# Two-layer hybrid decoder trunk with a mixture of experts: router matmuls turned around, top two by pairwise comparison, expert order and slots of the first expert moved ahead

## The reference

```python
def moe_ffn(x, w_router, wg, wu, wd):
    xt = x.reshape(B * S, D)
    logits = (xt @ w_router).astype(jnp.float32)
    top_v, top_i = lax.top_k(logits, TOP_K)
    w = jax.nn.softmax(top_v, axis=-1)
    gates = jnp.sum(jax.nn.one_hot(top_i, N_EXPERTS, dtype=jnp.float32) * w[..., None], axis=1)
    for e in range(N_EXPERTS):
        y = y + gates[:, e:e + 1].astype(xt.dtype) * swiglu(xt, wg[e], wu[e], wd[e])
```

## Time and profile before

| | |
|---|---|
| median of 3 runs | 1472.94 us (1471.33 to 1474.48) |
| the profiled execution's own time | 1472.44 us |
| its span | 1470.7 us |
| PE busy | 1396.2 us, 95% |
| DVE busy | 819.5 us, 56% |
| ACT busy | 705.5 us, 48% |
| DMA | 444.37 MB, mean 302 GB/s |
| chain that ended last | PE 86%, DVE 5%, ACT 4%, DMA 2% |

### The profile page before, as it was taken

How to read it: one execution, slowest core, us unless ns; L and a number is a source line. 1 busy time by engine, 2 the same in 40 slices (tenths; PEclk the granted TensorE clock), 3 DMA queues, 4 the chain that set the end, 5 groups by cost and what they waited for, 6 DMA issues and landing times.

```text
span 1470.7 us, 16634 instructions
## 1 busy us (share of the span) xinstructions
PE 1396.2 (95%) x6613; PEld 1012.9 (69%) x6613; DVE 819.5 (56%) x794; ACT 705.5 (48%) x773; POOL 35.9 (2%) x92
## 2 busy tenths in 40 slices
PE   8989999999899897999999999999999999999995
PEld 6865688888777746675756785757667757666574
DVE  4624454544354246655647675756656846547476
ACT  5454443444253523445635564545446645436363
POOL 2000000000000000000000000000000000000011
PEclk9989999999999897999999999999999999999998
DMA  9630755555343224999999999999999999999993
GB/s 342 224 115 1 258 199 180 192 174 176 137 148 126 104 86 158 410 409 409 402 409 410 403 393 394 409 411 409 409 396 410 410 409 403 409 410 409 402 403 128
DMA packets 148478, 444.37 MB, mean 302 GB/s; under 512 B 9454, under 2 KB 21612, under 8 KB 148396
## 3 DMA queue, kind: packets, MB, share of 16 engines
q1 hardware_dynamic: 146836, 438.24, 77.8%
q0 software_dynamic: 1440, 4.98, 0.8%
q10 hardware_dynamic: 120, 0.04, 0.0%
HBM read 439.30 MB, written 3.93 MB: 301 GB/s over the span
## 4 chain that ended last, share of the span: by engine, by line
PE 86%; DVE 5%; ACT 4%; DMA 2%; issue 1%; POOL 0%; DVEq 0%; POOLq 0%; SPq 0%; ACTq 0%
PE bank L821 83%; PE bank L824 3%; DVE ring_l L1772 1%; ACT part_h L1394 1%; DMA most<-in_moe_w_down_dram 1%; DMA ring<-in_moe_w_down_dram 1%; DVE most_l L1772 1%; DVE part_l L1772 0%; DVE more_l L1772 0%; ACT junk L1403 0%; ACT xh L1394 0%; ACT prob L1595 0%; DVE y L1772 0%; ACT probT L1394 0%; DVE gm L1777 0%
## 5 line engine op out<-in xcount | busy, mean ns | idle before, releaser
L1394 ACT ACTIVATE part_h<-ring 128x2048 fp32r<-128x2048 f32 x144 | 274.1, 1918 | 136.9 <-PE bank L821 132.4
L821 PE MATMUL bank<-part_h,xh 128*128 128x512 f32 x784 | 312.1, 398 | 6.1 <-DVE xl L2180 2.5
L821 PE MATMUL bank<-part_h,xl 128*128 128x512 f32 x784 | 306.2, 391 | 0.0
L1772 DVE TENSOR_TENSOR ring_l<-ring,part_h 128x2048 fp32r<-128x2048 f32 x102 | 231.6, 2289 | 49.5 <-ACT part_h L1394 48.7
L821 PEld LDWEIGHTS bank<-part_h,xh 128*128 128x128 f32 x784 | 147.6, 188 | 46.9 <-issue 8.2
L821 PE MATMUL bank<-part_h,hTh 128*128 128x512 f32 x392 | 156.2, 398 | 17.0 <-DVE ring_l L1772 10.2
L821 PEld LDWEIGHTS bank<-part_h,xl 128*128 128x128 f32 x784 | 147.5, 188 | 31.7
L821 PE MATMUL bank<-part_h,hTl 128*128 128x512 f32 x392 | 153.9, 393 | 0.0
L1772 DVE TENSOR_TENSOR part_l<-ring,part_h 128x2048 fp32r<-128x2048 f32 x42 | 96.1, 2292 | 83.8 <-ACT part_h L1394 83.8
L1772 DVE TENSOR_TENSOR part_l<-part_in,part_h 128x2048 fp32r<-128x2048 f32 x54 | 123.0, 2289 | 32.6 <-ACT part_h L1394 32.1
L821 PE MATMUL bank<-part_l,xh 128*128 128x512 f32 x360 | 140.2, 389 | 0.0
(11 more groups left out here) (320 smaller groups left out, 1837.9 us busy)
## 6 DMA issues: line engine op xcount, KB each, us to landing
ring<-in_moe_w_down_dram SPq DMA_DIRECT2D x60, 1024.0 KB, 13.9
ring<-in_moe_w_up_dram SPq DMA_DIRECT2D x58, 1024.0 KB, 14.7
ring<-in_moe_w_gate_dram SPq DMA_DIRECT2D x50, 1024.0 KB, 12.6
part_in<-in_moe_w_down_dram SPq DMA_DIRECT2D x36, 1024.0 KB, 14.0
most<-in_moe_w_gate_dram SPq DMA_DIRECT2D x27, 1024.0 KB, 14.8
part_in<-in_moe_w_up_dram SPq DMA_DIRECT2D x27, 1024.0 KB, 13.4
part_in<-in_moe_w_gate_dram SPq DMA_DIRECT2D x21, 1024.0 KB, 15.2
most<-in_moe_w_up_dram SPq DMA_DIRECT2D x17, 1024.0 KB, 13.2
```

Of the source, the lines that this page charges most:

```text
L821: return nc.tensor.matmul(o, lhsT, rhs, start=start, stop=stop)
L1394: return nc.scalar.activation(dst, src, ACT.Copy, scale=scale)
L1772: return nc.vector.tensor_tensor(o, a, b, op)
```

## The change

The router's weights, four times side by side and with the norm's gains multiplied in, become the stationary operand `w_r4` (32 columns, made once in the first layer by four VectorE operations); `xT` moves, 256 columns, and the eight products go to four column groups of the array, two into each. Evictions to `xT` are plain copies of 512 columns, two on each engine. The four partial sums are copied to SBUF (`lgT`) and two products with `fold` add them and turn them back. Six products whose result nobody reads stand between (`warm`). The best two of eight are found by comparing every pair of logits (`margin`, `beats`, `above`), without `rs`, which only the gap for the gates gets. Ranks and totals go to banks of their own, with two signals. `first_slots` builds expert 0's `gm` straight from ranks and selection; `gg` is built only for the last expert. The order of experts moves ahead of the first rows, `gates` and the third piece's split behind them, and `gates_shared` behind that. The first piece waits for half of the rows only (`m_xl`). The scaling of `xs` and one of the two squares change place or engine: ScalarE does the scaling, and squares block 0 before it evicts. The exponential moves behind ScalarE's first rows.

TensorE:

```diff
-                if l:
-                    pe.wait_ge(s_xTa, 4 * (3 * l + 2) + 4)
-                    pe.wait_ge(s_xTv, 4 * (3 * l + 2) + 4)
...
+            def warm(count):
+                for _ in range(count):
+                    mm(bank[7][:, :], part_h[:, 0, 0:P], part_h[:, 0, 0:W], True, True)
+            pe.wait_ge(s_wr, 1)
+            pe.wait_ge(s_hi, PIECES + 1)
+            t = 4 * (3 * (L - 1) + 2)
+            for i in range(KT // 2):
+                pe.wait_ge(s_xTv if i % 2 else s_xTa, t + 2 * (i // 2 + 1))
+                for k in (2 * i, 2 * i + 1):
+                    c = 32 * (k % 4)
+                    last = mm(bank[0][c:c + 32, 0:SEQ], w_r4[:, k, :], xT[:, k, :],
+                              k < 4, k >= 4)
+            last.then_inc(s_lp, 1)
+            warm(2)
+            pe.wait_ge(s_lt, 1)
             for b in range(NB):
-                for k in range(KT):
-                    i = mm(bank[0][:, b * E:(b + 1) * E], xT[:, k, b * P:(b + 1) * P], w_r[:, k, :],
-                           k == 0, k == KT - 1)
-            i.then_inc(s_lp, 1)
+                last = mm(bank[1][:, b * E:(b + 1) * E], lgT[:, b * P:(b + 1) * P], fold[:, 0:E], True, True)
+            last.then_inc(s_lp, 1)
+            warm(4)
...
+                    if (part, m) == (0, 0) and i * ks % (KT // 2) == 0:
+                        pe.wait_ge(m_xl, i * ks // (KT // 2) + 1)
```

VectorE (the first lines are in the first layer's mixer):

```diff
+                            for r in range(32 // E):
+                                i = tt(w_r4[:, :, r * E:(r + 1) * E], w_r[:, :, :],
+                                       cols[:, c_:c_ + KT, None].to_broadcast([P, KT, E]), ALU.mult)
+                            i.then_inc(s_wr, 1)
...
+            nc.vector.tensor_copy(lgT, bank[0][:, 0:SEQ]).then_inc(s_lt, 1)
...
+            dve.wait_ge(s_lp, 2)
+            link(nc.vector.tensor_copy(lg[:, :, :].rearrange("p b e -> p (b e)"), bank[1][:, 0:NB * E]))
+            for b in range(NB):
+                i = tt(margin[:, b], lg[:, b, None, :].to_broadcast([P, E, E]),
+                       lg[:, b, :, None].to_broadcast([P, E, E]), ALU.subtract)
+            link(i)
+            for b in range(NB):
+                i = tt(beats[:, b], margin[:, b], rank_hot[:, :, :], ALU.is_ge)
+            link(i)
+            link(nc.vector.tensor_reduce(above[:, :, :], beats, AX_X, ALU.add))
+            ts(rsg[:, 1], above[:, :, :], 2.0, None, ALU.is_lt).then_inc(s_sel, 1)
...
+            def first_slots():
+                dve.wait_ge(s_rk, 1)
+                link(nc.vector.tensor_copy(rsg[:, 0].rearrange("p b e -> p (b e)"), bank[2][:, 0:NB * E]))
+                for b in range(NB):
+                    ts(gm[:, b, :], iota_s[:, :], rsg[:, 0, b, 0:1], rsg[:, 1, b, 0:1],
+                       ALU.is_equal, ALU.mult).then_inc(m_first, 1)
...
+                    if shares:
+                        i = ts(gg[:, b, :], iota_s[:, :], col[:, b:b + 1], col[:, 2 * NB + b:2 * NB + b + 1],
+                               ALU.is_equal, ALU.mult)
...
-            slots(0, experts, m_gm)
+            first_slots()
+            expert_order()
+            moe_rows_low(0, 0)
+            moe_rows_low(0, 1)
+            gates()
             for j in AHEAD[1]:
                 split_moe(j)
-            moe_rows_low(0, 0)
-            moe_rows_low(0, 1)
+            gates_shared()
```

ScalarE:

```diff
                 if l:
-                    turned(3 * l + 2, "ffn", KT * l)
-                    block_squares()
+                    block_squares(0)
+                    turned(3 * l + 2)
+                    block_squares(1)
+                    act.wait_ge(s_xp, XB * (3 * l + 2))
+                    for b in range(NB):
+                        act.wait_ge(s_hrs, NB * l + b + 1)
+                        i = copy(xs[:, b, :], h[:, b, :], rs[:, b:b + 1])
+                    i.then_inc(s_xs, 1)
```

More of the change, by code:

```diff
@@ L15 @@
 NEG = -1e30
-HUGE = 3.0e38
+TINY = 1.2e-38
 NOPE, ROPE, HEADS = 64, 32, 4
@@ L1234, in gather_expert @@
             def gather_expert(e, r):
-                if e == 0 and r == 0:
-                    pe.wait_ge(s_xs, 1)
+                if e == 0:
+                    if r == 0:
+                        pe.wait_ge(s_xs, 1)
+                    for k in range(KT // 2):
+                        for b in range(NB):
+                            if r == 0 and k == 0:
+                                pe.wait_ge(m_first, b + 1)
+                            kk_ = KT // 2 * r + k
+                            last = mm(gather_bank(e, r)[:, k * P:(k + 1) * P], xs[:, b, kk_ * P:(kk_ + 1) * P],
+                                      gm[:, b, :], b == 0, b == NB - 1)
+                    last.then_inc(m_xep, 1)
+                    return
                 if r == 0:
-                    pe.wait_ge(m_gm, e + 1)
+                    pe.wait_ge(m_gm, e)
                 if e == 1:
@@ L1414, in mean_squares, with turned @@
                 squares_done(s_ms)
-            def turned(t, name, first):
-                for k in (0, 1, 4, 5):
+            def turned(t):
+                for k in (0, 4):
                     act.wait_ge(s_xp, XB * t + k // 2 + 1)
-                    copy(xT[:, k, :], bank[FFN_BANK[k // 2]][:, (k % 2) * SEQ:(k % 2 + 1) * SEQ],
-                         columns(name, first + k)).then_inc(s_xTa, 1)
+                    copy(xT[:, k:k + 2, :].rearrange("p k t -> p (k t)"),
+                         bank[FFN_BANK[k // 2]][:, :]).then_inc(s_xTa, 2)
             def split(f, j):
@@ L1832, in group_out, with turned @@
                        ALU.mult).then_inc(s_xTv, 1)
-            def turned(t, name, first):
-                for k in (2, 3, 6, 7):
+            def turned(t):
+                for k in (2, 6):
                     dve.wait_ge(s_xp, XB * t + k // 2 + 1)
-                    ts(xT[:, k, :], bank[FFN_BANK[k // 2]][:, (k % 2) * SEQ:(k % 2 + 1) * SEQ], columns(name, first + k), None,
-                       ALU.mult).then_inc(s_xTv, 1)
+                    nc.vector.tensor_copy(xT[:, k:k + 2, :].rearrange("p k t -> p (k t)"),
+                                          bank[FFN_BANK[k // 2]][:, :]).then_inc(s_xTv, 2)
             for l in range(L):
@@ L2058, in _ @@
                 if l:
-                    turned(3 * l + 2, "ffn", KT * l)
-                    scale_rows(l)
+                    turned(3 * l + 2)
                 else:
@@ new lines, in _ @@
+            link(ts(rank_hot[:, :, :], rank_hot[:, :, :], TINY, None, ALU.mult))
+            dve.wait_ge(s_lp, 2)
[4 more added lines that the diff above has]
+            link(i)
+            for b in range(NB):
+                i = tt(beats[:, b], margin[:, b], rank_hot[:, :, :], ALU.is_ge)
@@ new lines, in _, with gates @@
+            link(i)
+            link(nc.vector.tensor_reduce(above[:, :, :], beats, AX_X, ALU.add))
+            ts(rsg[:, 1], above[:, :, :], 2.0, None, ALU.is_lt).then_inc(s_sel, 1)
+            def gates():
+                for k in range(2):
+                    i = ts(oh[:, k], above[:, :, :], float(k), None, ALU.is_equal)
+                link(i)
+                for k in range(2):
+                    link(tt(rt_a[:, :, :], oh[:, k], lg[:, :, :], ALU.mult))
+                    link(nc.vector.tensor_reduce(top[:, k, :], rt_a[:, :, :], AX_X, ALU.add))
+                link(tt(gd[:, 0, :], top[:, 1, :], top[:, 0, :], ALU.subtract))
+                dve.wait_ge(s_hrs, NB * L)
+                tt(gd[:, 0, :], gd[:, 0, :], rs[:, 0:NB], ALU.mult).then_inc(s_lm, 1)
@@ L2136, in slots @@
+            def slots(n, key, done, shares):
+                n = n - 1
                 ts(eqm[:, :], key, cnt[:, 0:1], None, ALU.is_equal).then_inc(s_col, 1)
@@ L2287, in _ @@
                     dve.wait_ge(m_xep, rounds_before(e))
-                    slots(e, place[:, :], m_gm)
+                    slots(e, place[:, :], m_gm, e == E - 1)
                 if j in WIDE_N and EARLY <= j:
```

128 lines of the change are left out of this document (57 added, 71 removed).

## The result

| | before | changed |
|---|---|---|
| median | 1473.64 us (1471.33 to 1474.48, 4 runs) | 1462.51 us (1461.53 to 1465.13, 4 runs) |
| the profiled execution: own time, span | 1472.44, 1470.7 | 1461.96, 1460.1 |
| ratio, 95% interval | | 0.993 [0.9916, 0.9943] |

The changed kernel is faster by 0.7%. Between the profiled executions it is 10.5 us, where 14.6 were forecast.

A forecast was written before the change was run, and what follows sets the result against it. Near the end DMA decides, just before and after TensorE; the end moves by the smaller lead. TensorE's 12.8 at 850 us plus 1.8 of queue gives 14.6: 1472.44 - 14.6 = 1457.8 us, range 1454 to 1463.

The forecast's parts named there:

- TensorE's lead at the fifth piece: Expert stage: of 13.7 us gained at the first piece, 11.8 are left at the fifth, ready at 577.9.
- VectorE's queue: Behind the second half's rows: gate operations, `more_l`, caps and splits in turn, the fifth piece's split ready at 577.9.
- the reserve of 1.8 us: Load stream, 850 to 900 us: 1.8 us of queue left, added to TensorE's lead of 12.8, giving 14.6.
- the smaller of two leads: Near the end: TensorE and DMA must both move forward, and the end moves by the smaller of the two.
- the order (no change): SyncE's ordered loads: the order doesn't hold them, another wait does; about 1472 us, chance 0.02.
- half clock through the first pieces (slower): Expert stage: pieces at 1.2 GHz take 5.1 us, not 2.72; slower from the sixth on, 1475.6 us; chance 0.02.
- the queue does not limit: Load stream: with more reserve or TensorE lead, the end moves by SyncE's whole 17.7 us, to 1454.7; chance 0.12.
- Evictions, selection, ranks, expert order: Start of the changed part: evictions end 554.2, selection 557.2, second slot matrix 558.65, expert order 561.3, SyncE's loads 562.3.
- Gather and first piece: Both gather halves take 3.84 us at 2.4 GHz; the first piece starts at 563.15 instead of 576.81.
- the clock falls: Router to gather: TensorE's clock drops, 3.4 us less lead, 8.4 at the fifth piece, 1461.2 us; chance 0.24.
- The hole in DMA: Load stream near 590 us: queue empty for 2.1 us before the eleventh load, lead falling from 17.7 to 15.6.
- Small edits: Two fewer gate matrices save 0.52 us per slots build, two builds up to 850 us; first-layer multiplications cost 0 to 0.9.

The follow-up runs named there:

- load_wait3: The changed kernel with SyncE also waiting for the third piece's low part ahead of the loads that need the expert order; median 1464.17 us.
- warm_more: The changed kernel with ten unread products in TensorE's pauses around the ranks in place of six; median 1461.29 us.
- both_halves: The changed kernel with the first piece waiting for both halves of the rows again; median 1461.96 us.
- rest_later: The changed kernel with sixteen small VectorE operations on gates, caps and overflow moved behind the eighth piece's split; median 1460.11 us.
- gg_all: The changed kernel with the gate matrices `gg` built again for every expert from the second on; median 1464.58 us.

## Where the prediction failed, and why it was too large by 4 us

Two terms of the sum failed. The first is TensorE's lead at the fifth piece, put at 11.8 us and measured at 9.6: the gather was taken at 2.4 GHz and ran mostly at 1.2 (5.44 us against 3.84), and VectorE's queue made TensorE stop for 2.3 us ahead of the fourth piece, with the clock at 0.50 behind the stop, where the text had 0.9 us as the longest pause. The second is the reserve of 1.8 us that the stream was to give on top of TensorE's lead: none of it was there. The median of 1462.51 us lies inside the stated range, 0.5 under its upper end, but the forecast's sum did not bring it there.

**What bounds it: half of it shown.** The prediction has the end move by the smaller of two leads, that of TensorE and that of the loads. Over nine kernels the start of the loads moved by 8.6 to 17.3 us, and the end by 2.5 to 15.5, each time TensorE's lead at 850 us, within 0.7. The other half, an end held by the loads, showed in no run, and its premise failed: "a late start of that stream is never made up". In load_wait3 the loads led by 8.6 us and the end by 9.9. Rivals of the order (no change) and of half clock through the first pieces (slower) did not happen. Nor did the loads carry the end beyond TensorE's lead (the queue does not limit), and VectorE's sixteen small operations behind `more_l` took 3.2 us, as priced.

**Evictions, selection, ranks, expert order: right within 0.5 us.** Selection at 557.6 (557.2), second slot matrix at 559.1 (558.65), `order_i` at 561.7 (561.3), SyncE's loads at 562.64 (562.3). The router's sixteen instructions ran from 553.40 to 554.86 (554.7). The Trainium skill's warning that emptying PSUM may become the bottleneck (TensorEngine Tiling (Array Packing), Performance Considerations) agrees with the trace: the evictions set when the sixteen began, and the last four of them waited for the last eviction, which ended at 554.2. The sixteen took 1.46 us from first to last, and twelve of them lay under the evictions, as forecast.

**Gather and first piece: the clock.** I had 2.4 GHz from 553 to 563; it fell near 559.6 (0.78 in the window from 559 to 560), in a microsecond in which TensorE was busy for 0.98. 5.44 in place of 3.73 us, and the first piece at 564.75 in place of 563.15. That is the rival "the clock falls", by the sign that the prediction named for it, a clock at 0.50 at 560 us. Its price for the gather, 2.4, was too high, since the clock fell only after the first products; warm_more measures the whole fall at 1.7 us of the end. (The rival's time, 1461.2, is 0.8 from the profiled 1461.96, but that is luck, a sum of errors: 8.4 us at the fifth piece where 9.6 were left, and a reserve of 1.8 that was not there.) For the kernel before the prediction reads the first fall at 556.5; the window's 0.57 puts it at 556.1, and nothing hangs on it.

**VectorE's queue: a step that I did not finish.** The prediction has the third piece begin at 568.8 (its split) and the fourth piece's split end near 574.3 by its own terms (568.8 + 1.2 + 2.0 + 2.3). A piece lasts 2.72 us, so TensorE would stand still from 571.5 to 574.3, yet the text names 0.9 us as the longest pause. The sum to the fifth piece holds this pause, but at 2.4 GHz the fourth piece would have ended under VectorE's next split, so it cost nothing there; a fall of the clock behind it was not priced. In the trace it is 573.5 to 575.8, the clock is at 0.50 behind it, and the fourth piece ends later than VectorE's next split (579.18): so the fifth piece's lead is 9.6 and not 11.8. Of these 2.2 us, 1.3 are VectorE's queue, late by the slow gather (579.2 against the 577.9 forecast), and the rest the slow fourth piece. both_halves, where the clock stayed up, got 0.8 back, and rest_later, without queue or pause, 3.9. The Trainium skill (TensorE: Matmul & The Clock Gate, A second HAM failure mode: psum-queue depth-cycling) says that an engine which idles shortly and often between groups of matmuls loses and regains its clock again and again. The fall inside the gather, behind pauses of 0.65 and 0.30 us, may be of that kind; the second fall came behind one stop of 2.3 us, and what sets it off is not shown here.

**The hole in DMA: place right, size wrong.** The stream's lead, by the sums of GB/s, was 17.0 us ahead of 590 us and 12.6 behind it: a loss of 4.4 where 2.1 were forecast. The difference is again the fifth piece's 2.2 us, since the loads from the eleventh on wait for TensorE; load_wait3, whose loads start late, loses nothing there.

**Small edits: right.** The fifth piece's 9.6 became 10.6 at 850 us; gg_all, without them, stayed at 9.6 there. The four multiplications in the first layer cost nothing: at 540 us the two chains stand within 0.1 us.

**The reserve of 1.8 us: not there.** From 900 us on the changed kernel's stream leads by 11.3 with TensorE at 10.6, warm_more's by 12.7 with 12.1, rest_later's by 15.3 with 14.5. In all but load_wait3 the stream leads by TensorE's lead and 0.3 to 0.8, and at the end nearly all of it, or more, is given back. I had read the reserve from the shortest landing between 850 and 900 us, 6.8 against 5.0. A landing says how full the queue was at a load that was issued, not that loads came late; and the earlier trace rows show 393 and 394 GB/s in the slices from 846 to 919 us: before, too, the stream ran short there, so its queue did rest. After, a load in the same stretch lands as fast as a lone one:

```profile
DMA to landing us min/median/max: 5.0/8.0/14.9
```

The sum is thus 9.6 + 1.0 + 0.7 - 0.7 = 10.6 in place of 11.8 + 1.0 + 1.8 = 14.6: 2.2 by clock and pause, the rest by the reserve. rest_later, without the pause, has a lead of 13.5 at the fifth piece, 1.7 more than forecast, and of 14.6 at the end: the forecast's total by another sum, in which the missing reserve is made good by TensorE.

## What to carry to other kernels

Where a stream of loads and an engine may both hold the end, see by an experiment whose lead the end follows: halving the earlier start of the stream cost 0.7 us here, while sixteen small operations moved out of VectorE's way behind the first splits brought 4.1 by the profiles and 2.4 by the medians. Follow every engine's queue, piece by piece, through the whole start of a stage and write down the pauses that the sum itself contains, since a pause is a wait and may be a slower clock behind it. Products put into pauses must be tried in number: six did nothing, and with ten the clock stayed up.

## What the runs showed of the hardware that I had not expected

The clock may fall in the middle of an unbroken row of products (0.98 busy, then 0.50). It did so in seven profiles with six unread products or none, and in none of three with two more behind the ranks and two more ahead of them. These three are also the ones in which all of this came 3 to 7 us later in the execution, as told below, and no run separates the two.

A like difference, with the same instructions, lies far ahead of the change and makes most of what separates profiled executions. Windows of the kernel before:

```profile
80.00:84.00 4.00, 4.00 (x53) 3.21 (x52) 1.13 (x4) 0.00 (x0) 0.00 (x0) 1.00 0.01 4
84.00:88.00 4.00, 2.59 (x39) 1.63 (x37) 0.00 (x0) 3.20 (x9) 0.00 (x0) 1.00 0.93 335
```

and of warm_more, whose instructions are the same there:

```profile
80.00:84.00 4.00, 4.00 (x26) 3.22 (x29) 1.25 (x5) 0.00 (x0) 0.00 (x0) 0.50 0.02 4
84.00:88.00 4.00, 4.00 (x44) 2.63 (x40) 0.00 (x0) 0.05 (x1) 0.00 (x0) 0.81 0.13 30
```

After a stop at 76 to 80 us the clock is at 1.00 in the one and 0.50 in the other, and the mark lies at 552.42 and 558.42. Of these 6 us 4.5 are there soon behind that stop: VectorE's copy to `kcT` starts at 92.17 and at 96.71. Over the twelve profiles the mark stood at 551.9 to 552.4 five times, at 554.3 to 555.1 four times, and at 558.3 to 558.7 three times, these three being all the profiles with ten unread products. Whether code that runs 470 us later can have a part in that, or it is chance, no run here tells; the fastest timed runs of the same kernels (1456.03, 1459.26) don't show the 6 us. It is why differences of 1 to 2 us between medians of four runs were not read without the mark.
